# Ten modulation units and three rows of the opening on TensorE instead of VectorE and a trip through DRAM

## The reference, cut to what matters

```
c_act = silu(c)                                   # (1, 1024)
for l in range(2):
    mod = c_act @ ada_w[l] + ada_b[l]             # (1, 6 * 1024)
    shift_m, scale_m, gate_m, shift_f, scale_f, gate_f = split(mod, 6)
    h = rms_norm(x, g_pre_mix[l]) * (1 + scale_m) + shift_m
    q, k, v, u = split(h @ w_in[l] + b_in[l])
    attn_out = sliding_window_attention_with_sinks(rotary(q), rotary(k), v, sinks[l])
    pool_out = causal_pool_mixer(u, pool_w[l], pool_scale[l])
    mix = concat([attn_out, pool_out]) @ w_out[l]
    x = x + gate_m * rms_norm(mix, g_post_mix[l])
    h = rms_norm(x, g_pre_ffn[l]) * (1 + scale_f) + shift_f
    f = (silu(h @ w_gate[l]) * (h @ w_up[l])) @ w_down[l]
    x = x + gate_f * rms_norm(f, g_post_ffn[l])
```

## Time and profile before

| | us |
|---|---|
| median of 3 runs | 1273.38 |
| lowest, highest | 1272.33, 1275.3 |
| the profiled execution's own time | 1265.9 |
| its span, first to last instruction | 1264.1 |
| TensorE busy in the span | 1145.6 (91%) |
| VectorE busy | 842.0 (67%) |
| ScalarE busy | 644.2 (51%) |
| weights and other data read from DRAM | 253.79 MB, 202 GB/s over the span |

### The profile page before, as it was taken

One profiled execution on the slowest core, in us unless ns is written; L12 is line 12 of the kernel. 1 busy time (PEld: TensorE's weight loads), 2 busy tenths in 40 slices (PEclk: granted clock), 3 DMA queues, 4 the chain that ended last, 5 costly groups with the idle time before them and its releaser, 6 DMA issues.

```text
span 1264.1 us, 19698 instructions
## 1 busy us (share of the span) xinstructions
PE 1145.6 (91%) x7883; PEld 1041.7 (82%) x7883; DVE 842.0 (67%) x1324; ACT 644.2 (51%) x1126; POOL 53.8 (4%) x73
## 2 busy tenths in 40 slices
PE   2759299999985989999999999999999999999998
PEld 2547299999874789999988879999989878999996
DVE  4897587877786466555567666765667756765664
ACT  4433363434543564444475566655456566654553
POOL 3200100000010010000000000000000000000000
PEclk9978699999997999999999999999999999999999
DMA  7978669999759237668644234555553523465540
GB/s 288 327 279 214 204 256 303 356 258 373 289 143 257 85 134 276 209 231 235 219 142 180 101 134 161 208 193 192 180 190 128 194 92 136 157 217 192 178 164 34
DMA packets 38363, 256.16 MB, mean 203 GB/s; under 512 B 4704, under 2 KB 4992, under 8 KB 9984
## 3 DMA queue, kind: packets, MB, share of 16 engines
q1 hardware_dynamic: 34416, 242.50, 56.8%
q0 software_dynamic: 3136, 10.42, 2.4%
q10 hardware_dynamic: 720, 1.97, 0.4%
HBM read 253.79 MB, written 1.09 MB: 202 GB/s over the span
## 4 chain that ended last, share of the span: by engine, by line
PE 73%; DVE 11%; DMA 7%; ACT 4%; issue 3%; POOL 1%; ACTq 0%; DVEq 0%; POOLq 0%
PE bank L473 23%; PE bank L475 23%; PE bank L474 23%; DMA raw_w<-weights 5%; DVE lo_w L1380 3%; PE bank L480 2%; DVE raw_w L1390 2%; DMA start<-positions 1%; ACT gtok L1047 1%; DVE in_lo L1470 1%; DMA sinks<-sink_rows 1%; ACT hi_w L1041 1%; DVE prob L1490 1%; DVE smax L1493 1%; PE bank L520 1%
## 5 line engine op out<-in xcount | busy, mean ns | idle before, releaser
L1380 DVE TENSOR_TENSOR lo_w<-raw_w,hi_w 128x1024 fp32r<-128x1024 f32 (+4 forms) x370 | 433.0, 1192 | 155.0 <-ACT hi_w L1041 154.1
L1041 ACT ACTIVATE hi_w<-raw_w 128x1024 fp32r<-128x1024 f32 (+4 forms) x370 | 370.5, 1026 | 194.1 <-DMA raw_w<-weights 98.9
L473 PE MATMUL bank<-in_hi,lo_w 128*128 128x256 f32 x1408 | 395.7, 281 | 0.0
L474 PE MATMUL bank<-in_lo,hi_w 128*128 128x256 f32 x1408 | 393.0, 279 | 0.0
L475 PE MATMUL bank<-in_hi,hi_w 128*128 128x256 f32 x1408 | 392.9, 279 | 0.0
L473 PEld LDWEIGHTS bank<-in_hi,lo_w 128*128 128x128 f32 x1408 | 264.3, 188 | 2.5 <-issue 0.8
L474 PEld LDWEIGHTS bank<-in_lo,hi_w 128*128 128x128 f32 x1408 | 263.7, 187 | 1.9 <-issue 0.5
L475 PEld LDWEIGHTS bank<-in_hi,hi_w 128*128 128x128 f32 x1408 | 264.6, 188 | 0.0
L473 PE MATMUL bank<-hi_w,in_lo 128*128 128x256 f32 (+2 forms) x544 | 178.1, 327 | 29.8 <-DVE in_lo L1541 12.3
L474 PE MATMUL bank<-lo_w,in_hi 128*128 128x256 f32 (+2 forms) x544 | 174.6, 321 | 0.0
L475 PE MATMUL bank<-hi_w,in_hi 128*128 128x256 f32 (+2 forms) x544 | 174.4, 321 | 0.0
(11 more groups left out here) (200 smaller groups left out, 1011.9 us busy)
## 6 DMA issues: line engine op xcount, KB each, us to landing
raw_w<-weights SPq DMA_DIRECT2D x219, 1024.0 KB, 5.0
raw_w<-weights SPq DMA_DIRECT2D x8, 640.0 KB, 6.2
rows<-mod_rows POOLq DMA_DIRECT2D x10, 512.0 KB, 8.8
rows<-norm_rows POOLq DMA_DIRECT2D x5, 512.0 KB, 5.0
raw_w<-weights SPq DMA_DIRECT2D x2, 832.0 KB, 4.4
const<-const_table SPq DMA_DIRECT2D x1, 1538.0 KB, 8.1
raw_w<-weights SPq DMA_DIRECT2D x2, 768.0 KB, 4.6
shared<-bias_rows POOLq DMA_DIRECT2D x2, 640.0 KB, 10.4
```

Source lines behind the costliest of these rows:

```text
L473: nc.tensor.matmul(o, st[1], mv[0], start=start, stop=False, **kw)
L474: nc.tensor.matmul(o, st[0], mv[1], start=False, stop=False, **kw)
L1041: nc.scalar.activation(hi_w[:, m % NSPLIT, cut], raw_view(unit)[:, cut], ACT.Identity).then_inc(*sig("hi_w", unit, i))
L1380: nc.vector.tensor_tensor(lo_w[:, m % NSPLIT, cut], raw_view(unit)[:, cut], hi_w[:, m % NSPLIT, cut].bitcast(F32), ALU.subtract).then_inc( ...
```

## The change

1. Units 0 to 3, 8 to 11, 16 and 17 of layer 0 go to TensorE. Their weights are packed untransposed; `ada_columns` multiplies each of the 16 blocks of 128 x 128 as stationary operand with one column of the condition as moving operand, into one column of a bank. VectorE only copies two columns out (`ada_in`). The condition as a column comes through the vector transposes at the start (it is put at the head of `VECTORS`), with its own silu on ScalarE.
2. The rows gate of the mixer, scale and shift of the feed-forward (layer 0) are spread on TensorE: a column of `modcol`, repeated 128 times, is the stationary operand and the identity the moving one; ScalarE copies the two banks into `rows` (`spread_row`, `row_in`). Their three trips through DRAM go. The seven other rows keep theirs.
3. Units are ordered j, 4+j; ScalarE's queue loads vectors and constants first; ScalarE prepares both `ink` units of a round before the tiles' high parts; banks are renumbered; the first bias load waits for unit 3's matmuls in place of VectorE's unit 7; the load of layer 1's bias moves ahead of the first `scale`; layer 1's shift row goes ahead of its scale row, and three waits for `scaled` go.

```diff
+PE_ADA = {(0, n) for n in (0, 1, 2, 3, 8, 9, 10, 11, 16, 17)}
-        for n in (4 + j, j):
+        for n in (j, 4 + j):
+            def ada_columns(l, n, bank):
+                unit = ("ada", l, n)
+                pe.wait_ge(*due(f"raw_w{UNIT_NO[unit] % NRAW}", unit))
+                b = take(("ada_cols", unit), bank)
+                w = raw_view(unit).rearrange("p (t c) -> p t c", t=KT)
+                for f in range(2):
+                    for t in range(KT):
+                        last = nc.tensor.matmul(b[:, f:f + 1], w[:, t, P * f:P * (f + 1)], ccol[:, t:t + 1], start=(t == 0), stop=(t == KT - 1))
+                last.then_inc(*sig("ada_cols", unit))
+            def spread_row(L, kind, w):
+                pe.wait_ge(*due("modcol", L, kind, w))
+                for c in range(2):
+                    job = ("spread", L, kind, w, c)
+                    b = take(job)
+                    for i in range(4):
+                        t = 4 * c + i
+                        last = nc.tensor.matmul(b[:, P * i:P * (i + 1)], modcol[:, ROWS[(L, kind, w)], t:t + 1].to_broadcast([P, P]), k("ident"),
+                                                start=True, stop=True)
+                    last.then_inc(*sig(*job))
@@ TensorE, ending @@
                 into_y(L, w, other, 0, last=True)
+                if opening:
+                    banks(4, 5, 6, 7)
+                    spread_row(0, "scale", 1)
                 into_y(L, w, one, 1)
...
                     into_y(L, w, other, 1, last=True)
+                    if opening:
+                        spread_row(0, "shift", 1)
                     turn_norm(N, 0)
@@ TensorE, input product of layer 0 @@
                         done.then_inc(*sig("used", ("ink", 0, kk)))
+                        if kk % 2 == 0:
+                            ada_columns(0, 1 + kk // 2, 6 + (1 + kk // 2) % 2)
...
                     scores_late()
+                    ada_columns(0, 8, 4)
...
+                if L == 0:
+                    ada_columns(0, 9, 5)
                 turn_prob(0)
                 turn_prob(1)
+                if L == 0:
+                    ada_columns(0, 10, 4)
...
+                if L == 0:
+                    ada_columns(0, 11, 5)
                 for n in range(3, 6):
                     turn_prob(n)
+                if L == 0:
+                    ada_columns(0, 16, 4)
+                    ada_columns(0, 17, 5)
...
                     attention(q)
+                if L == 0:
+                    spread_row(0, "gate", 0)
@@ GpSimd @@
-            pool.wait_ge(*due("ada", ("ada", 0, 7)))
+            pool.wait_ge(*due("ada_cols", ("ada", 0, 3)))
             load(bias, a_bias[0:1, :], 1280, "bias_in", 0)
...
-            mod_row(0, "gate", 0)
-            mod_row(0, "scale", 1)
-            mod_row(0, "shift", 1)
+            pool.wait_ge(*due("tok", 0, 1, 2))
+            load(bias, a_bias[1:2, :], 1280, "bias_in", 1)
             scale(("ffn", 0), 0, 0)
@@ VectorE @@
                 for j in range(4):
                     if j > 0:
                         ada(0, 4 + j)
-                    ada(0, j)
-                    ve.wait_ge(*due("ada", ("ada", 0, j)))
+                    ada_in(0, j)
+                    ve.wait_ge(*due("ada_in", ("ada", 0, j)))
...
-                    if L == 0 and n == 1:
-                        ada(0, 10)
...
-                    if L == 0 and n in (3, 4, 5):
-                        ada(0, (11, 16, 17)[n - 3])
+                    if L == 0 and n in (2, 3, 4, 5):
+                        ada_in(0, 6 + n)
+                        if n == 5:
+                            row_columns(0, 2)
...
                 if L == 0:
                     lo(("wo", 0, 0))
+                    ada_in(0, 16)
+                    ada_in(0, 17)
                     ada(0, 18)
```

More of the change, by code:

```diff
@@ L632, in slice_of @@
                                      start=(kk == 0), stop=(kk == KT - 1))
-                    for T, c in places:
-                        take(("in", 0, T, c))
+                    for n, (T, c) in enumerate(places):
+                        take(("in", 0, T, c), n)
                     for kk in range(6):
@@ L886, in _ @@
             pe.wait_ge(*due("vec_in", 0))
-            transposes(("vec",), [vrow[:, P * g:P * (g + 1)] for g in range(NVEC)])
+            take(("vec",), 7)
+            for g in range(NVEC):
+                last = nc.tensor.transpose(ps(("vec",))[:, P * g:P * (g + 1)], vrow[:, P * g:P * (g + 1)], k("ident"))
+            last.then_inc(*sig("vec"))
+            pe.wait_ge(*due("ccol", 0))
+            ada_columns(0, 0, 6)
             for T in range(2):
@@ L978, in scale @@
                         pool.wait_ge(*due("x", L, w, T, c))
-                        if T == 0 and c == 0:
-                            pool.wait_ge(*due("row1", N[1], "scale", 0 if N[0] == "mix" else 1))
+                        if T == 0:
+                            row = (N[1], "scale", 0 if N[0] == "mix" else 1)
+                            if row != (0, "scale", 1):
+                                pool.wait_ge(*due("row1", *row))
+                            else:
+                                pool.wait_ge(*due("row", *row, c))
                         if T == 1:
@@ L992, in _ @@
             mod_row(0, "gate", 1)
-            pool.wait_ge(*due("scaled", ("ffn", 0), 1, 1))
+            mod_row(1, "shift", 0)
             mod_row(1, "scale", 0)
-            mod_row(1, "shift", 0)
-            pool.wait_ge(*due("tok", 0, 1, 2))
-            load(bias, a_bias[1:2, :], 1280, "bias_in", 1)
             scale(("mix", 1), 0, 1)
@@ L1066, in chain @@
                 prepare(following, (0,))
+                if (L, w, T) == (0, 0, 0):
+                    row_in(0, "shift", 1)
                 for c in range(2):
@@ L1069, in chain, with row_in @@
                 prepare(following, (1,))
+            def row_in(L, kind, w):
+                slot = ("gate", "scale", "shift").index(kind)
+                for c in range(2):
+                    copy(("spread", L, kind, w, c), rows[:, slot, cols(c)], ps(("spread", L, kind, w, c))[:, :], "row", L, kind, w, c)
             def by_tile(bank):
@@ L1368, in in_turn @@
             def in_turn(unit):
+                while UNITS[taken[0]][0][0] == "ada" and UNITS[taken[0]][0][1:] in PE_ADA:
+                    taken[0] += 1
                 assert UNITS[taken[0]][0] == unit, (unit, UNITS[taken[0]][0])
@@ L1393, in ada, with row_columns, ada_in @@
                 if n % 4 == 3 and not (l == 0 and n < 8):
-                    ve.wait_ge(*due("ada", unit))
-                    g = n // 4
-                    kind, w_ = ("shift", "scale", "gate")[g % 3], g // 3
-                    mod_column(l, kind, w_, 8 * g, 0, 8, modcol[:, ROWS[(l, kind, w_)], :]).then_inc(*sig("modcol", l, kind, w_))
+                    row_columns(l, n // 4)
+            def row_columns(l, g):
+                for m in range(4 * g, 4 * g + 4):
+                    ve.wait_ge(*due("ada_in" if (l, m) in PE_ADA else "ada", ("ada", l, m)))
+                kind, w = ("shift", "scale", "gate")[g % 3], g // 3
+                mod_column(l, kind, w, 8 * g, 0, 8, modcol[:, ROWS[(l, kind, w)], :]).then_inc(*sig("modcol", l, kind, w))
+            def ada_in(l, n):
+                unit = ("ada", l, n)
+                ve.wait_ge(*due("ada_cols", unit))
+                nc.vector.tensor_copy(mods[:, l, 2 * n:2 * n + 2], ps(("ada_cols", unit))[:, 0:2]).then_inc(*sig("ada_in", unit, frees=("ada_cols", unit)))
             def mod_column(l, kind, w, at, a, b, dst):
@@ L1411, in behind @@
                 for n in ADA_AFTER.get(unit, ()):
-                    ada(*n)
+                    if n not in PE_ADA:
+                        ada(*n)
             def residual(L, w, T):
@@ L1421, in residual @@
                     return
-                ve.wait_ge(*due("row0", L, "gate", w))
+                if (L, w) != (0, 0):
+                    ve.wait_ge(*due("row0", L, "gate", w))
                 for c in range(2):
+                    if (L, w) == (0, 0):
+                        ve.wait_ge(*due("row", 0, "gate", 0, c))
                     job = ("y", L, w, T, c)
@@ L1633, in attention_windowed @@
                                                 ALU.subtract).then_inc(*sig("cat_lo", L, t, frees=("attn", L, jp)))
-                behind(("wo", L, 1))
+                if L == 0:
+                    for n in (13, 14, 15):
+                        ada(0, n)
                 lo(("gu", L, 0))
```

91 lines of the change are left out of this document (55 added, 36 removed).

## The result

| | before | changed |
|---|---|---|
| median of 15 runs each | 1271.77 | 1280.87 |
| lowest, highest | 1268.31, 1275.8 | 1275.34, 1289.85 |
| the profiled execution's span | 1264.1 | 1277.2 |

The ratio of changed to before is 1.0072 (95% interval 1.0052 to 1.0092), so the change makes the kernel slower, by 9.1 us. The direction was forecast, the size was not: the prediction's sum came to 1295.4, +22.0.

A forecast was written before the change was run, and what follows sets the result against it. Limits differ by stage: TensorE and VectorE alternating, VectorE in the attention, TensorE in the output product, then the shift row's trip. 11 + 26.4 + 3.8 - 19.2 = +22.0 us gave 1295.4; range 1258 to 1303.

The forecast's parts named there:

- Input product, +11 forecast: Input product: three blocks between TensorE's slices delay the bias and sinks load, and so the evacuation, by +11 us.
- Attention, +26.4 forecast: Attention: six units queue on TensorE, mostly at the low clock, making the stage 58.8 us against 32.4, +26.4.
- The ends of the bound: A unit's block on TensorE: 3.5 us at the high clock from below, 6.8 at the low clock from above.
- Rows and the end: Output product: two row spreads add +3.8 us; behind it, 5.0 us in place of 24.2 before the feed-forward, -19.2.
- A: Rival, all blocks: the stream of weight loads keeps TensorE at the high clock; about -10.5 us, 1263; chance 0.30.
- B: Rival: the clock holds in the input product but not in the attention; +15 us, 1288; chance 0.13.
- C: Rival: a load's time doesn't depend on the clock, so blocks are 3.5 us everywhere; 0, 1273; chance 0.06.
- D: Rival: a block costs more than 6.8 us, draining before the array's weights change; +31 or more, 1304; chance 0.08.
- the likeliest case: Whole kernel: blocks run half or wholly at the low clock; +22.0 us, 1295.4, own range 1286 to 1302; chance 0.43.
- The slices of rows 1: Profile page's slices of the span: TensorE read as 9 tenths busy nearly throughout, lower only in the first five, some 158 us.
- the angles as late as before: Input product's start: angles and sine come as late as before, so round 1 gains nothing.

The follow-up runs named there:

- columns alone: Changed kernel with its three spread rows going by way of DRAM again, ten units still on TensorE; ratio 1.023 against the kernel before.
- last six: Changed kernel with units 0 to 3 back on VectorE, only units 8 to 11, 16 and 17 on TensorE; ratio 0.9992 against the kernel before.
- bias early: Changed kernel with the bias and sinks load waiting for unit 1's columns instead of unit 3's; ratio 1.0048 against the kernel before.
- kernel without columns: Changed kernel with all 24 units on VectorE, the three rows still spread by TensorE; ratio 0.9887 against the kernel before.
- kernel that has the rows by way of DRAM: Changed kernel with no unit on TensorE and the three rows through DRAM, only the rest of the change left; ratio 0.9997 against the kernel before.
- 128 columns: Changed kernel with the condition's column repeated 128 times as moving operand in each unit's products; ratio 0.9927 against the kernel before.
- 32 columns: Changed kernel with the condition's column repeated 32 times as moving operand in each unit's products; ratio 1.0024 against the kernel before.

## Why the prediction was right in direction and wrong in size

**Input product, +11 forecast, +15.7 measured.** The path was right: unit 3's block, then the load of bias and sinks, then the evacuation. Three steps on it were off.

- The block. It was forecast to end at 64.2 and ended at 65.2. The blocks were cheaper than assumed (4.18, 4.22 and 4.25 us for 5.1; from start to start 12.2 in place of 15.3), and the five slices ahead of it dearer, 25.4 us for 18 + 3.4. The first of them took 6.1 where 3.6 stood in the sum: its matmuls of 512 columns take 0.43 us from one to the next until 33.07, and 0.23 from there. It was low in the kernel before too, where the same slice took 5.2 us (26.78 to 31.96). The other four took 19.3 for 17.8, low until 43.3 behind the first block.
- The load. Its transfer was assumed to be a little shorter and was longer, 10.47 us for 9.21: 2.0 us later than forecast, the evacuation at 76.80 for 74.
- From the evacuation to the scores it is 8.8 us, with the last tile's first matmuls at the low level, where the kernel before took 7.1.

1.0 + 2.0 + 1.7 = 4.7, the miss. The kernel with the columns alone has the same order there, and its trace has the scores at 81.49, +11.6. So the miss is no larger than the difference between two executions, and not much should be built on it. The load sets the evacuation, but with a cover of 1.3 us only.

**Attention, +26.4 forecast, +13.4 measured.** This is the term that was mis-sized. Two steps of it failed. First, the blocks: 5.1 + 5 x 6.8 = 39.1 us were assumed, as if the clock stayed low once it had fallen; it comes back in the pool's products, and the blocks took 31.8. The ends of the bound were right, 3.65 and 6.98 us for 3.5 and 6.8; how many lie at which end was not. Second, TensorE's other work: 16.2 + 2.6 + 0.9 = 19.7 us were assumed and 14.0 measured (45.8 less 31.8). The gaps of 2.6 us are filled, and work that had been at the low level before, behind gaps, is in part at the high one. Together 7.3 + 5.7 = 13.0, which is the whole miss of this stage. The other traces with six blocks of one column (columns alone, last six, bias early) have the last pair wholly low and the stage at 50.6, 48.9 and 48.9 us, with blocks of 35.2, 34.8 and 34.8 and other work of 15.3, 14.1 and 14.1. So the blocks' part of the miss is 4 to 7 us by the execution, the other part 4 to 6, and the term was too high in all four.

**Rows and the end.** +3.8 forecast and 3.8 measured (31.7 us from the output product to the shift's spread at 163.12, against 27.9); 5.0 for 24.2 us forecast, 5.3 measured. The kernel without columns shows the two by themselves: its feed-forward starts 16.3 us before that of the kernel that has the rows by way of DRAM (140.86, 157.18), for 15.4 by the forecast's two terms.

Sum of the misses: 4.7 - 13.0 + 0.3 = -8.0, and 22.0 - 8.0 is the 14.0 by which the feed-forward starts later. From there to the end the changed kernel gains 0.9 (span +13.1). The medians differ by 9.1: the profiled execution of the kernel before was 5.9 us under the median of its 15 runs and that of the changed one 1.9 under its own. So of the 13 us between 22 and 9, eight are the terms, one lies later, and four are which executions were recorded. That it was not more is partly luck: the misses of the two stages have opposite signs.

**The rivals.** A needed blocks of 4.5 us on average; they took 5.15 (51.5 us for ten). With 128 columns its case comes true, and gives 1.2 us less than it said (-9.3 for -10.5); that this is so close is luck in part, since the evacuation was at 69.90 for its 67, the output product at 112.00 for 108 and the feed-forward at 147.22 for 143. B was right in form for 32 columns: the clock holds in the input product and not in the attention. With one column neither stage held it. C, a load's time without the clock: out, 32 loads took 6.98 us with a granted clock of 0.50 and 3.65 with 1.00. D, blocks of more than 6.8 us: 6.98 and 6.99 were the longest, so 0.22 us a load, the bound from above and nothing more.

The range (1258 to 1303) held the time, and the likeliest case's own (1286 to 1302) missed it by 5 us: each stage lay between the cases, while the forecast had only their ends. The range reached over A's middle too, from 15 us faster to 30 slower than before, so that it held says little.

**A reading that was wrong and cost nothing.** The slices of rows 1 are low not only in the first five: the 12th, 13th and 15th read 8, 5 and 8. The changed kernel reads 8, 5, 8, 8 from the 12th on; nothing of the change lies there.

**A load at either clock.** In the blocks, with nothing to cover the load, a load of 128 columns takes 3.65 / 32 = 0.114 us at the granted clock of 1.00 and 6.98 / 32 = 0.218 at 0.50. The Trainium skill, in "TensorE: Matmul & The Clock Gate", section LDWEIGHTS, gives columns over 1.2, so 107 ns for 128 columns: the trace agrees at the high level and disagrees at the low one, where it is twice that.

## What to carry to other kernels

A matrix-vector product on TensorE is a stream of weight loads: price it at both clock levels, per stage, and look at the granted clock beside the busy share, since an engine without one idle microsecond ran two thirds of a stage at half speed here. If such a stream has to be there, let the vector be repeated over more moving columns and look at the clock again: 128 of them gave back 18 us here, 32 only 6. Before two edits are judged as one, take them apart: one gained 14 us, the other lost 24.

## What was not expected of the hardware

**Columns that move, and the clock.** Blocks with one moving column and blocks with 128 have the same loads and the same busy engine; the clock over the attention was 0.67 with the one and 1.00 with the other, and the block went from 6.98 to 3.84 us. The same 32 columns held it in one stage (0.93) and not in the next (0.66).

**GpSimd beside VectorE.** The angles' chain on GpSimd took 16.5 us before (19.34 to 35.85) and 9.4 in the changed kernel (16.84 to 26.27), with the same instructions. Before, GpSimd's and, below, VectorE's order of time:

```profile
21.49 1.05 POOL L945 TENSOR_SCALAR start<-start 128x16 f32<-128x16 f32 x1
22.62 1.07 POOL L947 TENSOR_SCALAR start<-start 128x16 f32<-128x16 f32 x1
```

```profile
21.21 1.22 DVE L1390 SCALAR_TENSOR_TENSOR raw_w<-raw_w,c_row 128x1024 f32<-128x1024 f32 x1
...
22.36 1.21 DVE L1390 SCALAR_TENSOR_TENSOR raw_w<-raw_w,c_row 128x1024 f32<-128x1024 f32 x1
```

and the same two of GpSimd's in the changed kernel, in which VectorE has no unit there:

```profile
18.57 0.26 POOL L1001 TENSOR_SCALAR start<-start 128x16 f32<-128x16 f32 x1
18.91 0.26 POOL L1003 TENSOR_SCALAR start<-start 128x16 f32<-128x16 f32 x1
```

1.05 and 1.07 us against 0.26 each, while VectorE reads `raw_w` and `c_row`. The Trainium skill, in "SBUF — State Buffer", section "SBUF: two separate sides", says that a VectorE operation with two inputs in SBUF holds the port that the two engines share for its whole length, against a GpSimd operation that reads SBUF. The trace agrees: GpSimd's two operations start within VectorE's and end at 22.54 and 23.69, 0.1 us behind the end of VectorE's at 22.43 and 23.57. Before, ScalarE's sine waited 0.74 us for the chain and ran at 35.89; in the changed kernel it waited for nothing of it and still ran at 36.47. So the 7 us gave nothing; the forecast had the angles as late as before, which was wrong and cost it nothing.
